# First products of the compressed branch in eight steps of four, and what follows five visits later

## The reference

```python
def compress_blocks(t, pe, w1, w2):
    b, s, hk, d = t.shape
    n_cmp = (s - CMP_BLOCK) // CMP_STRIDE + 1
    idx = np.arange(n_cmp)[:, None] * CMP_STRIDE + np.arange(CMP_BLOCK)[None, :]
    blk = jnp.swapaxes(t[:, idx], 2, 3) + pe
    blk = blk.reshape(b, n_cmp, hk, CMP_BLOCK * d)
    return jax.nn.gelu(blk @ w1) @ w2
...
    kc = compress_blocks(k_c, cmp_pe_k, cmp_w1_k, cmp_w2_k)
    vc = compress_blocks(v_c, cmp_pe_v, cmp_w1_v, cmp_w2_v)
    s_cmp = jnp.einsum('bshgd,bchd->bhgsc', qg, kc) * scale
    cmp_end = jnp.arange(n_cmp) * CMP_STRIDE + CMP_BLOCK - 1
    cmp_valid = cmp_end[None, :] <= t_pos[:, None]
    p_cmp = masked_softmax(s_cmp, cmp_valid) * jnp.any(cmp_valid, axis=-1)[:, None].astype(jnp.float32)
    o_cmp = jnp.einsum('bhgsc,bchd->bshgd', p_cmp, vc.astype(jnp.float32))
```

## Time and profile before

| | |
|---|---|
| time before, median of three runs | 2410.18 us (2407.19 to 2411.22) |
| profiled execution: its own time | 2413.85 us |
| its span | 2412.5 us |
| TensorE matmul (PE) busy | 2365.5 us, 98% |
| VectorE (DVE) busy | 1376.8 us, 57% |
| ScalarE (ACT) busy | 1164.0 us, 48% |
| GpSimd (POOL) busy | 9.6 us |
| DMA moved | 400.13 MB, 166 GB/s on average |

### The profile page before, as it was taken

How to read it: one execution, slowest core, us unless ns; L and a number is a source line. 1 busy time by engine, 2 the same in 40 slices (tenths; PEclk the granted TensorE clock), 3 DMA queues, 4 the chain that set the end, 5 groups by cost and what they waited for, 6 DMA issues and landing times.

```text
span 2412.5 us, 27677 instructions
## 1 busy us (share of the span) xinstructions
PE 2365.5 (98%) x11308; PEld 1939.6 (80%) x11308; DVE 1376.8 (57%) x1962; ACT 1164.0 (48%) x1641; POOL 9.6 (0%) x17
## 2 busy tenths in 40 slices
PE   8999999999999999999999999999999999999997
PEld 6788888888788888887787888888888888888886
DVE  5676554666555585586645555655454454444554
ACT  5456654555654653353335554445444344434443
POOL 0000000000000000000000000000000000000000
PEclk9999999999999999999989999999999999999999
DMA  7354445554545542342444445555555555555552
GB/s 262 131 175 144 153 157 192 175 175 155 168 167 178 171 146 88 106 139 88 157 140 140 157 144 177 185 192 192 192 184 185 192 190 192 192 185 192 186 186 105
DMA packets 204271, 400.13 MB, mean 166 GB/s; under 512 B 12656, under 2 KB 12816, under 8 KB 203760
## 3 DMA queue, kind: packets, MB, share of 16 engines
q1 hardware_dynamic: 201920, 391.08, 48.0%
q0 software_dynamic: 1648, 6.32, 0.9%
q10 hardware_dynamic: 576, 0.95, 0.1%
HBM read 396.23 MB, written 2.10 MB: 165 GB/s over the span
## 4 chain that ended last, share of the span: by engine, by line
PE 92%; DVE 4%; ACT 3%; issue 1%; DMA 0%; ACTq 0%; DVEq 0%
PE ACC L797 27%; PE ACC L799 26%; PE ACC L798 26%; PE TP L428 2%; ACT arena L820 1%; DVE WL L1671 1%; PE SC L677 1%; PE PV L623 1%; PE TP L473 1%; PE SC L618 1%; PE SC L465 1%; PE PV L626 1%; PE PV L651 1%; ACT WH L820 0%; ACT L820 0%
## 5 line engine op out<-in xcount | busy, mean ns | idle before, releaser
L1671 DVE TENSOR_TENSOR WL<-W,WH 128x1024 fp32r<-128x1024 f32 x740 | 901.0, 1220 | 654.8 <-ACT WH L820 653.4
L820 ACT ACTIVATE WH<-W 128x1024 fp32r<-128x1024 f32 x740 | 781.2, 1056 | 858.3 <-PE ACC L799 853.1
L797 PE MATMUL ACC<-WH,XH 128*128 128x512 f32 x2592 | 1047.9, 404 | 7.1 <-ACT arena L820 6.1
L799 PE MATMUL ACC<-WH,XL 128*128 128x512 f32 x2592 | 1014.9, 392 | 0.0
L798 PE MATMUL ACC<-WL,XH 128*128 128x512 f32 x2592 | 1012.9, 391 | 0.0
L797 PEld LDWEIGHTS ACC<-WH,XH 128*128 128x128 f32 x2592 | 489.0, 189 | 120.4 <-issue 18.6
L799 PEld LDWEIGHTS ACC<-WH,XL 128*128 128x128 f32 x2592 | 487.9, 188 | 106.0
L798 PEld LDWEIGHTS ACC<-WL,XH 128*128 128x128 f32 x2592 | 489.4, 189 | 92.0 <-issue 1.0
L797 PE MATMUL ACC<-WH,HH 128*128 128x512 f32 x352 | 139.5, 396 | 0.0
L799 PE MATMUL ACC<-WH,HL 128*128 128x512 f32 x352 | 138.2, 393 | 0.0
L798 PE MATMUL ACC<-WL,HH 128*128 128x512 f32 x352 | 137.0, 389 | 0.0
(11 more groups left out here) (259 smaller groups left out, 1496.2 us busy)
## 6 DMA issues: line engine op xcount, KB each, us to landing
W<-in_w_in SPq DMA_DIRECT2D x84, 1024.0 KB, 4.8
W<-in_a_w_in SPq DMA_DIRECT2D x48, 1024.0 KB, 5.1
W<-in_w_ffn_gate SPq DMA_DIRECT2D x44, 1024.0 KB, 5.0
W<-in_w_ffn_up SPq DMA_DIRECT2D x44, 1024.0 KB, 5.1
W<-in_w_ffn_down SPq DMA_DIRECT2D x44, 1024.0 KB, 5.1
W<-in_b_w_in SPq DMA_DIRECT2D x40, 1024.0 KB, 5.0
W<-in_a_w_out SPq DMA_DIRECT2D x16, 1024.0 KB, 5.0
W<-in_b_w_out SPq DMA_DIRECT2D x16, 1024.0 KB, 5.0
```

The lines of the kernel that those rows point to most:

```text
L797: MM(out, hx, WH[:, k, 0:ch.width], start=q == 0 and k == 0, stop=False)
L799: ins = MM(out, lx, WH[:, k, 0:ch.width], start=False, stop=last and k == QK - 1)
L820: return nc.scalar.activation(out, in_, func, **how)
L1671: TT(tiles_of(M.WL[n % 2], ch, half), tiles_of(M.W[n % 4], ch, half), tiles_of(M.WH[n % 2], ch, half).bitcast(F32), ALU.subtract).then_inc ...
```

## The change

The 32 first products of each compression are issued four to a visit, on eight visits, where they were eight to a visit on four. ScalarE's generator yields ten times in place of six, so that the Gelu stays one visit behind the last product. The second compression begins two visits later, `compressed` five visits later, the first attention at K+39 (was K+34: five later) and the second at K+88 (was K+84: four later). The instructions are the same in number and kind; only their places in the order of each engine move.

```diff
@@ -244,11 +244,11 @@
         begin(after(f"c.kv{i}") + 1, "nsa_rope", 2 * i)
     begin(after("c.kv2") + 7, "nsa_keys")
     begin(after("c.kv2") + 5, "compress", 0)
-    begin(after("c.kv2") + 22, "compress", 1)
-    begin(after("c.kv2") + 29, "compressed")
+    begin(after("c.kv2") + 24, "compress", 1)
+    begin(after("c.kv2") + 34, "compressed")
     for g in range(2):
         begin(after(f"c.nq{g}"), "nsa_queries", g)
-        begin(after("c.nq1") + 2 + 50 * g, "nsa_attend", g)
+        begin(after("c.nq1") + 7 + 49 * g, "nsa_attend", g)
     for c in range(2):
         begin(first("c.mg7") + 4 * (c + 1), "turn", "on.c", c)
         begin(first("c.mg7") + 4 * (c + 3), "turn", "od.c", c)
@@ -675,7 +675,7 @@
         pe.wait_ge(*at("blocks_laid", j))
         for n in range(32):
             ins = MM(SC[j][:, 0:2 * NC2], M.W1[:, n, :], M.BL[:, n, :], start=n == 0, stop=n == 31)
-            if n % 8 == 7:
+            if n % 4 == 3:
                 if n == 31:
                     ins.then_inc(*did("hidden_multiplied", j))
                 yield
@@ -1051,7 +1051,7 @@
             yield
 
     def compress(j):
-        for _ in range(6):
+        for _ in range(10):
             yield
         act.wait_ge(*at("hidden_multiplied", j))
         A(M.H1[j], SC[j][:, 0:2 * NC2], ACT.Gelu_apprx_tanh).then_inc(*did("hidden_activated", j))
```

## The result

The changed kernel takes 2418.55 us, the median of 8 runs (2414.27 to 2422.51), beside 2410.21 for 8 runs of the kernel before (2407.19 to 2413.03). The ratio is 1.0038, with a 95% interval of 1.0027 to 1.0048: slower by 0.38%, clear of noise. The forecast was 2418.0. The profiled execution took 2418.47 us. Of the runs further down, one execution of e7_split_36_84 took 8410.36 us, for a reason that nothing here shows, and its ratio leaves it out.

A forecast was written before the change was run, and what follows sets the result against it. TensorE, busy 98% of the span, was taken as the bound. 2401.9 us without clock falls, + 1.0 switches + 9.0 waits = 2411.9, plus clock loss 8.3 - 5 + 2.5 = 5.8, gave 2417.7, so 2418; range 2409 to 2426.

The forecast's parts named there:

- waits at the attentions: Behind visit K, first after chunk c.kv2: TensorE's waits for ScalarE's table loads grow from 4.0 to 13.05 us, +9.0.
- wait for the blocks: Before the first compression's first burst: TensorE's 1.94 us wait for VectorE's laying of the blocks stays.
- The switches: Eight more visits mix small products with large matmuls, each costing 0.12 us: +1.0 us, between 0 and 2.
- The clock at the first compression: Thinner bursts give back 5 of the 8.3 us a typical run loses to the low clock.
- New falls of the clock: At the attentions, two new TensorE waits of 2.5 and 3.2 us may lower the clock: +2.5 us, 0 to 5.
- The second weight load: POOL queue's second 2 MB load, waiting for hidden 0, stays hidden with some 4.6 us to spare: cost 0.
- A: Rival: thinned bursts and new waits never let the clock fall; 2411.9 us, faster if added waits stay small; chance 0.18.
- B: Rival: at the first compression the clock falls anyway and stays low over eight visits; 2433 us; chance 0.06.
- C: Rival: the second weight load comes late, crowded by the weight stream; 2421 us if 3 us beyond its slack; chance 0.04.
- D: Rival: nothing of note at the attentions, each group's waits trade places; 2409 us; chance 0.10.

The follow-up runs named there:

- e7_split_36_84: Changed kernel (products split four to a visit) with the attentions begun at K+36 and K+84 instead of K+39 and K+88; 2405.97 us, ratio 0.9990 to the kernel before.
- e1: Kernel before with only the change's later order (second compression, compressed step, attentions), products still eight to a visit; 2418.61 us, ratio 1.0042.
- e3: Changed kernel with the eight merge chunks taken by a copy instead of a Sigmoid; 2402.45 us, ratio 0.9972 to the kernel before.
- e5: Kernel before with only the second attention moved, to K+88 from K+84; 2414.16 us, ratio 1.0026.
- e2: Changed kernel's split products, but the attentions kept at K+34 and K+84 as in the kernel before; 2407.75 us, ratio 0.9993 to the kernel before.
- e4: Kernel before with the eight merge chunks taken by a copy instead of a Sigmoid; 2401.73 us, ratio 0.9973.
- e6: Kernel before with TensorE asking for the first compression's blocks at K+9 instead of K+7; 2404.50 us, ratio 0.9976.
- e8: Kernel before asking for the first blocks at K+9 instead of K+7 and beginning the first attention at K+35 instead of K+34; 2402.88 us, ratio 0.9973.

## Why the prediction was right

**Direction and size.** 2418.0 was forecast, 2418.55 measured, in the middle of the range. The total rests on one large term that held and on smaller ones that were off and happened to cancel, which was luck. With what the profiles show, the sum is 2401.9 without falls, + 0.2 for the split, + 8.9 for the waits at the attentions, - 0.3 for a shorter wait for the blocks, + 7.9 for the clock = 2418.6, where the profiled execution took 2418.47 and the forecast had 1.0, 9.0, 0 and 5.8. The switches were 0.8 us too high and the clock 2.1 too low.

**The waits at the attentions (+9.0).** This step held, wait by wait. Forecast and measured: K+48 0.85 and 0.85; K+63 3.2 and 3.15; K+81 1.5 and 1.76; K+96 0.85 and 0.85; K+103 0.2 and 0.22; K+112 0.85 and 1.8, 0.83 and 1.63; K+121 0.2 and under 0.15; K+127 2.5 and 2.49; K+130 0.25 and 0.31; K+144 0.85 and 0.85. The sum is 13.05 against 12.94. The count of loads held as well, three more at either line. It worked because the trace of before already held every pattern of take, load and exponential that the new order would make, so that only places had to be worked out. e1, e3 and e5 show that these waits, and the loads behind them, are the cause.

**The switches (+1.0).** Wrong: I charged 0.12 us of slower large matmuls for each added burst, and put each half burst at half of the whole. It is shorter: two halves take 2 x 0.81 us against 1.70, which gives most of the 0.12 back. Two visits cost 4.57 in place of 4.54: 0.03 for each of eight pairs, 0.2 us in all.

**The clock at the first compression (-5).** The mechanism was right and the size too large. e2 puts the split, clock and all, at 0.5 us in the median and 2.0 in the mean. I had taken most of a typical run's 8.3 us of lost clock to lie at 1202, where the profile showed 10.3. But that profile was one of the slower executions. The profiles of e1, e4 and e5, with the same wait and bursts, have no fall at 1202; they have two short ones at 1165 and 1175, which the profile of before lacks. And the 8.3 came from three runs; by the medians of the later sets it is 5 to 6.

**New falls of the clock (+2.5).** One was seen, 6.8 us long and worth 2.9, in the 3.15 us wait; e1's profile has one at the same place, worth 1.7. From e2 to the change 2.6 us are left that its waits don't explain, which agrees. How often each of the two waits brings a fall, the few profiles don't show.

**The wait for the blocks** stayed, as said, but a little shorter (1.62 us in this execution for 1.94).

**The second weight load** was hidden: issued at 1220.78 and landing 11.0 us later, at 1231.8, with the first product that needs it at 1236.72. That leaves 4.9 us; I had 4.6.

**The rivals.** A, the clock decides: no. The new waits came, and what the split spares of the clock is 0.5 us in the median and 2.0 in the mean (e2), too little to outweigh them. The Trainium skill, "TensorE: Matmul & The Clock Gate", section "Loop structure matters more than you think", has the clock stay up where matmuls follow each other without a wait for data. This case's traces agree in part: most such stretches ran at full clock, but the clock also fell at 1165, behind 4.6 us in which TensorE never waited. B, low over eight visits: seen in no run, and no split run had a mean clock under 0.993. C: no, as just said. D: e7 is D made true by placing, and took 2406 where I had 2409.

The Trainium skill, "ScalarE: Activation LUTs", section "What ACT_TABLE_LOAD costs", has a drain beside each load. None is seen here either: the take at 1306.23 follows 1.30 us behind the load of 1.28. Going by the row was right; with two drains by the page's figure, the K+63 wait would have been near 6 us, by my estimate, and it was 3.15.

**Open:** the change's own 8.3 us over the kernel before in its comparison and the 10.4 of e1 in its set differ by 2 us, for kernels with the same median; the median of the kernel before moved (2410.2, 2408.2, 2407.8, 2406.7 in four sets). That its runs follow their granted clock (2405.4 us on average at 0.996, 2414.4 at 0.992) makes the clock the likely reason, but what sets it from run to run was not tried.

## What to carry to other kernels

Where one engine takes results at fixed places and does side work in between with another function table, a side task's start is chosen modulo the chunk: write down at which of the chunk's steps each of its exponentials falls, and keep them off the takes and the step behind them. Moving such a task by three to five steps "out of the way" can cost more than the thing it makes room for. And before thinning a burst to help the clock, look for the wait in front of it: removing that was worth 3.3 us here, thinning the burst about 2 in the mean. That a wait stands in front is worth checking first, but it is not the only thing that brings the clock down (1165).

## What I had not expected of the hardware

- A burst of small float32 products can be cut in two between large matmuls at no cost: 4.57 against 4.54 us for two visits.
- The same kernel, run again, spreads over 12 us (2404.27 to 2416.89 in 31 runs) in step with its mean granted clock, 0.998 to 0.991. A single profile can show a fall of 20.5 us that a typical run doesn't have.
- The clock fell without any wait of TensorE in front: at 1165 and 1175 in the changed kernel's profile, behind bursts of small matmuls. Of the eleven profiles seven have these two falls, e6 and e7 have two like them behind an earlier pass over the same lines, and before and e8 have none.
- At the first compression, small differences in the wait went with the fall. In the eight profiles that have the wait for the blocks, it lasts 1.62 or 1.63 us in six, and the clock holds; it lasts 1.94 (before) and 1.92 (e7) in two, and the clock falls. The six are those with the falls at 1165 and 1175. This was seen, not tried.
- Of two waits of nearly the same length in one profile (3.15 and 2.49 us) the clock fell in the first alone, and in e5's profile it fell around 1428, at a wait of the same 2.49 us at the same K+127. The same wait brings a fall in one execution and none in another. Windows of e5, the wait and what follows it:

```profile
1424.00:1427.60 3.60, 1.11 (x11) 1.06 (x10) 1.10 (x5) 3.55 (x7) 0.00 (x0) 0.99 0.00 0
1427.60:1431.00 3.40, 3.40 (x10) 2.67 (x9) 2.26 (x6) 3.37 (x5) 0.00 (x0) 0.50 0.02 5
```
